# A two-block network on one core: the end of the first feed-forward, the place of memory's first key and value products, and the order inside three residual loops

## The chip, the core and the metric

One Trainium2 chip, one of its cores, one launch. The metric is the device time of the program in microseconds (us), lower is better. The core has five engines that each run their own instruction list and meet through semaphores: TensorE (PE) multiplies, VectorE (DVE), ScalarE (ACT) and GpSimd (POOL) do elementwise work, SyncE (SP) issues the weight loads.

## What is computed

Two blocks in a row on 256 tokens of width 1024, in float32. The first block ends with a feed-forward over a 3x3 convolution; the second has a mixer, an attention over 256 memory tokens, and a feed-forward. Cut to what matters here:

```python
# first block, its end
x = x + mx[:, :, 5] * conv_ffn(h2, ffn_up, ffn_conv_w, ffn_conv_b, ffn_down, rows, GRID_W)
x = rmsnorm(x, final_g)
# second block
h = rms_norm(x, norm_mix_w)
x = x + hybrid_mixer(h, w_in, pool_w, pool_scale, gk_w2, gk_b, gla_norm_w, w_out)
h = rms_norm(x, norm_xattn_w)
m = rms_norm(mem, norm_mem_w)
x = x + memory_cross_attention(h, m, wq, wkv, wo)     # keys m @ wk, values m @ wv
h = rms_norm(x, norm_ffn_w)
x = x + conv_ffn_2(h, w_up, conv_w, conv_b, w_down)
x = rms_norm(x, norm_final_w)
```

The keys and values of memory depend on `mem` alone, so their products can stand anywhere before the attention.

## The kernel before, in words

**Weights in two halves.** Every product is made of three TensorE passes, to keep float32's digits: high weights by high input, low weights by high input, high weights by low input. Weights come in chunks of 128x1024 (512 KB). `CHUNKS`, made by `chunk_list`, is their one order, and every engine follows it. SP loads chunk j into `raw`, ACT copies it, rounded, into `whi` (`splits`, line 1164), and DVE or POOL subtracts to get `wlo` (`low_half`, line 492; which of the two is `LOW_BY`). All three rings hold four chunks (`RAW`, `HL`): ACT may make the high half of chunk j only when TensorE has finished chunk j-4, and SP may load chunk j only when the low half of j-4 is made.

**One chunk on TensorE** is 24 matmuls: eight k tiles by three passes (`lin`, lines 625, 627, 629). `lins` takes three chunks side by side, one k tile after another. A feed-forward's down chunk (`slab`, lines 948 to 952) adds one k tile to all eight output columns, which lie in four banks; `slabs` does this for two chunks with the eight columns as the outer loop, so that the first columns are ready while the later ones are still being computed. `lin_tok` computes a chunk pair of the values with tokens as rows.

**Residual loops.** `residual(name)` runs over the eight columns j of a projection that is added to x. DVE adds the product to x (`xT`), ACT makes the high half of the next input (`h2h`, line 1388), DVE the low half (`h2l`, line 1572), ACT the squares (`sq`), DVE their sum (`ssum`). Between these stand the weights' halves of coming chunks. The names are `down` (end of the first feed-forward), `w_out2` (end of the mixer) and `wo` (end of the attention); the next products, `w_in2`, `wq` and `up2`, read `h2h` and `h2l` by k tile. The root mean square is not needed for these products: `means` sums the squares on TensorE, ACT takes the root, DVE inverts it, `spread` puts it on all partitions by a small matmul, and the products are scaled by it afterwards.

**Around the change.** TensorE ends the first feed-forward with down chunks 19 and 20 (counted from 0), memory's key columns 4 and 5 (`wk`), down chunk 21, and the pair of chunks of memory's values 0 (`wv`), then `w_in2`. Later, after the mixer's head products (lines 1058 and 1059), it takes the means of the heads (`g0`, `g1`), spreads the first block's root (`rs1`), computes key columns 6 and 7, spreads `mem`, and goes to `w_out2`. The last attention head is computed after the value chunks 6 and 7, and then `wo`.

## Time and profile before

| | |
|---|---|
| median of 3 runs | 893.72 us (891.81 to 894.41) |
| the profiled execution | 894.42 us |
| its span, first to last instruction | 892.6 us |
| PE, matmuls busy | 858.7 us (96%) |
| DVE busy | 583.2 us (65%) |
| ACT busy | 462.7 us (52%) |
| POOL busy | 441.5 us (49%) |
| mean granted TensorE clock | 0.985 |

The span is the part that the trace covers; 1.8 us of the profiled execution lie outside it. Matmul ends are modelled, so the spacing of their starts tells more than their busy time. A granted clock of 1.00 is TensorE's upper level (2.4 GHz), 0.50 the lower (1.2 GHz). A row's idle time, in square brackets, is what its engine waited before it, with the one that released it.

### The profile page before, as it was taken

How to read it: one execution, taken by the hardware profiler on the slowest of the kernel's cores; microseconds unless marked ns; L12 is line 12 of the kernel's file. 1: busy time of each engine (PE TensorE's matmuls, PEld its weight loads, DVE VectorE, ACT ScalarE, POOL GpSimd, SP SyncE). 2: the span in 40 equal slices, each digit the busy share in tenths (PEclk: the TensorE clock that was granted, in tenths of full speed). 3: DMA queues.
4: the chain of work that ended last, by engine and by line, in shares of the span. 5: the costliest groups of instructions: out<-in, count | busy, mean ns of one | idle time of the engine just before them, and what ended most of it. 6: DMA issues, size and time to landing. Idle time of an engine off the chain costs nothing.

```text
span 892.6 us, 16215 instructions
## 1 busy us (share of the span) xinstructions
PE 858.7 (96%) x6572; PEld 818.5 (92%) x6572; DVE 583.2 (65%) x1182; ACT 462.7 (52%) x753; POOL 441.5 (49%) x217
## 2 busy tenths in 40 slices
PE   6799999999999999999999899899999999999996
PEld 2388999998899999999999899899999999999996
DVE  6988987866767796776765769676458433433335
ACT  5332344542656665555554664455445555545555
POOL 0766412222652798888888100000003688787882
PEclk9899999999999999999999999899999999999998
DMA  9957574655375466565565446154535475655651
GB/s 344 350 210 247 181 236 163 225 166 185 134 239 187 145 191 192 182 189 184 176 187 182 134 127 204 53 167 133 174 98 163 123 211 181 187 177 186 189 166 48
DMA packets 45758, 160.95 MB, mean 180 GB/s; under 512 B 5218, under 2 KB 5490, under 8 KB 45556
## 3 DMA queue, kind: packets, MB, share of 16 engines
q1 hardware_dynamic: 45680, 159.91, 55.6%
q8 instruction: 52, 0.85, 0.4%
q14 instruction: 22, 0.18, 0.1%
q10 hardware_dynamic: 4, 0.01, 0.0%
HBM read 158.85 MB, written 1.05 MB: 179 GB/s over the span
## 4 chain that ended last, share of the span: by engine, by line
PE 78%; DVE 11%; ACT 4%; issue 3%; DMA 2%; POOL 1%; SPq 0%; DVEq 0%; ACTq 0%; POOLq 0%
PE bank L629 16%; PE bank L625 16%; PE bank L627 16%; PE bank L952 4%; PE bank L950 4%; PE bank L948 4%; DVE wlo L492 3%; ACT whi L1164 2%; PE bank L753 2%; PE bank L837 2%; DMA ada_kT<-in_adaT 1%; PE bank L705 1%; PE bank L694 1%; PE bank L690 1%; PE bank L692 1%
## 5 line engine op out<-in xcount | busy, mean ns | idle before, releaser
L492 POOL TENSOR_TENSOR wlo<-raw,whi 128x1024 fp32r<-128x1024 f32 (+1 forms) x177 | 411.9, 2348 | 392.2 <-ACT whi L1164 392.1
L1164 ACT ACTIVATE whi<-raw 128x1024 fp32r<-128x1024 f32 (+1 forms) x253 | 258.3, 1026 | 78.6 <-PE bank L629 41.7
L629 PE MATMUL bank<-h2l,whi 128*128 128x256 f32 x848 | 240.9, 284 | 2.4 <-DVE h2l L1572 2.4
L625 PE MATMUL bank<-h2h,whi 128*128 128x256 f32 x848 | 242.2, 286 | 0.5 <-ACT h2h L1388 0.5
L627 PE MATMUL bank<-h2h,wlo 128*128 128x256 f32 x848 | 240.4, 284 | 0.0
L1572 DVE SCALAR_TENSOR_TENSOR accs<-bank,vec,accs 128x189 f32<-128x189 f32 (+4 forms) x440 | 161.1, 432 | 72.3 <-ACT accs L1434 72.3
L629 PEld LDWEIGHTS bank<-h2l,whi 128*128 128x128 f32 x848 | 163.2, 192 | 3.5 <-DVE h2l L1572 3.5
L625 PEld LDWEIGHTS bank<-h2h,whi 128*128 128x128 f32 x848 | 163.3, 193 | 1.4 <-ACT h2h L1388 0.7
L627 PEld LDWEIGHTS bank<-h2h,wlo 128*128 128x128 f32 x848 | 163.3, 193 | 0.1
L492 DVE TENSOR_TENSOR wlo<-raw,whi 128x1024 fp32r<-128x1024 f32 x76 | 92.5, 1226 | 26.8 <-ACT whi L1164 26.3
L952 PE MATMUL bank<-gl,whi 128*128 128x256 f32 x336 | 95.2, 283 | 1.3 <-DVE gl L1569 1.3
L950 PE MATMUL bank<-gh,wlo 128*128 128x256 f32 x336 | 95.1, 283 | 0.0
L948 PE MATMUL bank<-gh,whi 128*128 128x256 f32 x336 | 95.1, 283 | 0.0
L1434 ACT ACTIVATE accs<-bank,vec 128x256 f32<-128x256 f32 x88 | 44.9, 561 | 86.7 <-DVE bank L1569 53.3
L1569 DVE TENSOR_TENSOR bank<-bank,rsd 128x256 f32<-128x256 f32 x44 | 16.8, 428 | 89.1 <-PE bank L629 89.1
L625 PE MATMUL bank<-hch,whi 128*128 128x256 f32 (+1 forms) x240 | 73.5, 306 | 0.0
L627 PE MATMUL bank<-hch,wlo 128*128 128x256 f32 (+1 forms) x240 | 73.0, 304 | 0.0
L629 PE MATMUL bank<-hcl,whi 128*128 128x256 f32 (+1 forms) x240 | 73.0, 304 | 0.0
L952 PEld LDWEIGHTS bank<-gl,whi 128*128 128x128 f32 x336 | 64.5, 192 | 1.5 <-DVE gl L1569 1.5
L948 PEld LDWEIGHTS bank<-gh,whi 128*128 128x128 f32 x336 | 64.5, 192 | 0.0
L950 PEld LDWEIGHTS bank<-gh,wlo 128*128 128x128 f32 x336 | 64.5, 192 | 0.0
L629 PEld LDWEIGHTS bank<-hcl,whi 128*128 128x128 f32 x240 | 45.8, 191 | 1.9
(328 smaller groups left out, 1689.0 us busy)
## 6 DMA issues: line engine op xcount, KB each, us to landing
raw<-in_up SPq DMA_DIRECT2D x88, 512.0 KB, 3.6
raw<-in_w_in SPq DMA_DIRECT2D x45, 512.0 KB, 3.7
raw<-in_down SPq DMA_DIRECT2D x44, 512.0 KB, 3.6
ada_kT<-in_adaT SPq DMA_DIRECT2D x22, 512.0 KB, 4.0
raw<-in_w_out SPq DMA_DIRECT2D x16, 512.0 KB, 4.3
raw<-in_w_in_t SPq DMA_DIRECT2D x12, 512.0 KB, 4.6
ada_vM<-in_adaT SPq DMA_DIRECT2D x10, 512.0 KB, 4.3
ada_buf<-in_adaT SPq DMA_DIRECT2D x8, 512.0 KB, 10.5
```

Source lines behind the costliest of these rows:

```text
L492: return e.tensor_tensor(wlo[:, j % HL, 0:k], raw[:, j % RAW, 0:k], whi[:, j % HL, 0:k].bitcast(F32), ALU.subtract)
L625: e.matmul(ps, wh[:, k, :], xh(k), start=k == 0, stop=False)
L627: e.matmul(ps, wl[:, k, :], xh(k), start=False, stop=False)
L629: t = e.matmul(ps, wh[:, k, :], xl(k), start=False, stop=k == KTILES[name] - 1)
L753: t = e.matmul(rows[h][0:2, :], M["cs"][:, k, :], M["ada_sc"][:, k, h * 512:h * 512 + 512], start=k == 0, stop=k == KT - 1)
L837: t = e.matmul(banks[4 + slot][:, h * 128:h * 128 + 128], M["near"][:, h, tile], by_blocks(Q2, h, tile, 1 << v), start=True, stop=True)
L948: e.matmul(ps, wh[:, j, :], gh, start=k == 0 and j % 2 == 0, stop=False, skip_group_check=True)
L950: e.matmul(ps, wl[:, j, :], gh, start=False, stop=False, skip_group_check=True)
L952: t = e.matmul(ps, wh[:, j, :], gl, start=False, stop=k == NFF - 1, skip_group_check=True)
L1164: e.activation(whi[:, j % HL, 0:(k1 - k0) * 128], raw[:, j % RAW, 0:(k1 - k0) * 128], ACT.Copy).then_inc(S.hi.up(j))
L1434: e.activation(acc_at(t), z_at(f, t), ACT.Identity, scale=conv_weight(f, n, centred(f)), bias=conv_bias(f, n)).then_inc(S.acc0.up((f, t)))
L1572: return e.scalar_tensor_tensor(out=out, in0=a, scalar=s, in1=b, op0=o1, op1=o2)
```

## The change

On TensorE, down chunks 20 and 21 are now computed together, by columns, with key column 4 ahead of them and key column 5 behind them; values 0 move from there to a place behind key column 7, before `w_out2`. The first `w_in2` chunks are computed one after another and not three side by side. The `rs1` spread and key column 6 go ahead of the heads' means, and DVE inverts their roots after it has scaled x. Part of the low halves changes engine: `w_in2` 16 goes from DVE to POOL, and `up2` 0, 22 and 1 from POOL to DVE. In the loops `w_out2` and `wo`, ACT makes the high half of chunk j+4 first, before it waits for the new x of column j, and DVE adds product j to x before the low half of chunk j+4, where that low half used to stand behind `h2l` of column j and ahead of the next addition. The last head's transposes (`turn(3)`) go between the two value chunks 6 and 7.

```diff
@@ chunk_list
-            elif i == NFF + DLAG - 1:
+            elif i == NFF + DLAG - 2:
                 for name, n in beside:
                     one(name, n)
...
-    ffn("up", "down", [("wk", 4), ("wk", 5)])
-    two("wv", 0)
+    ffn("up", "down", [("wk", 4)])
+    one("wk", 5)
...
     for j in (6, 7):
         one("wk", j)
+    two("wv", 0)
@@ low_by
-        if name in ("up", "down", "up2", "down2") or (name == "wk" and n in (4, 5)) or (name == "wv" and n < 2):
+        if name == "up2" and n in (0, 1, NFF):
+            out.append("dve")
+        elif name in ("up", "down", "up2", "down2") or (name == "wk" and n in (4, 5)) or (name == "wv" and n < 2):
+            out.append("pool")
+        elif (name, n) == ("w_in2", 16):
             out.append("pool")
@@ TensorE's list
-            for k in range(NFF - DLAG, NFF - 1):
-                slab(0, "down", k)
+            slab(0, "down", NFF - 3)
             mem_key(4)
+            slabs(0, "down", (NFF - 2, NFF - 1))
             mem_key(5)
-            slab(0, "down", NFF - 1)
-            mem_value(0)
...
-            for n in range(2):
-                means(f"g{n}", sq_at(("heads", 1, n)), 4, S.sqo, f"g{n}", (S.yb, (1, 2 * n + 1)), 1)
...
-            mem_key(6, lambda: [spread(f"g{n}", aux_bank(f"g{n}")) for n in range(2)])
-            mem_key(7)
+            mem_key(6)
+            for n in range(2):
+                means(f"g{n}", sq_at(("heads", 1, n)), 4, S.sqo, f"g{n}", (S.yb, (1, 2 * n + 1)), 1)
+            mem_key(7, lambda: [spread(f"g{n}", aux_bank(f"g{n}")) for n in range(2)])
+            mem_value(0)
...
-            mem_value(3)
-            turn(3)
+            mem_value(3, lambda: turn(3))
@@ ScalarE's residual
+                    if name in ("w_out2", "wo"):
+                        if j < 7:
+                            splits(ch(name, j) + HL + 1)
+                        else:
+                            sqrt_next()
                     if name in AHEAD:
...
-                        if j < 7:
-                            splits(ch(name, j + 1) + HL)
-                        if j == 7:
-                            sqrt_next()
                         squares(name, j, xT[:, j, :])
@@ VectorE's residual
-                        los(ch(name, j) + HL)
+                        if j == 0:
+                            los(ch(name, 0) + HL)
                         w.wait_ge(S.chunk, ch(name, j))
...
                         if name in AHEAD:
+                            if j < 7:
+                                los(ch(name, j) + HL + 1)
                             low(j)
```

**DVE in the residual loop `down`.** Rows of DVE's list, behind the last `gl` of the first feed-forward; `wlo` rows are weights' low halves. Before:

```order
L1572 SCALAR_TENSOR_TENSOR xT<-bank,mod,xT 128x256 [waits s_summed,s_ada]
L1572 SCALAR_TENSOR_TENSOR xT<-bank,mod,xT 128x256
L1572 SCALAR_TENSOR_TENSOR xT<-bank,mod,xT 128x256 [waits s_summed]
L1572 SCALAR_TENSOR_TENSOR h2l<-xT,fgm,h2h 128x256 [waits s_xh]
L1572 SCALAR_TENSOR_TENSOR xT<-bank,mod,xT 128x256
L1572 SCALAR_TENSOR_TENSOR h2l<-xT,fgm,h2h 128x256 [waits s_xh]
L1572 SCALAR_TENSOR_TENSOR xT<-bank,mod,xT 128x256 [waits s_summed]
L1572 SCALAR_TENSOR_TENSOR h2l<-xT,fgm,h2h 128x256 [waits s_xh]
L492 TENSOR_TENSOR wlo<-raw,whi 128x1024 [waits s_hi]
```

Now:

```order
L1579 SCALAR_TENSOR_TENSOR xT<-bank,mod,xT 128x256 [waits s_summed]
L1579 SCALAR_TENSOR_TENSOR xT<-bank,mod,xT 128x256
L1579 SCALAR_TENSOR_TENSOR h2l<-xT,fgm,h2h 128x256 [waits s_xh] x2
L1579 SCALAR_TENSOR_TENSOR xT<-bank,mod,xT 128x256 [waits s_chunk]
L1579 SCALAR_TENSOR_TENSOR xT<-bank,mod,xT 128x256
L1579 SCALAR_TENSOR_TENSOR h2l<-xT,fgm,h2h 128x256 [waits s_xh] x4
L497 TENSOR_TENSOR wlo<-raw,whi 128x1024 [waits s_hi]
L1576 TENSOR_TENSOR ssum<-ssum,sq 128x512 [waits s_sqr]
```

The additions now go in pairs with the low halves of the input in pairs behind them, and the weights' low half that stood among them (`w_in2` 16) is gone from DVE; the next one (`w_in2` 4) stands behind the last `h2l`.

**DVE from the memory keys into the loop `w_out2`.** Rows from the last products of the mixer's heads on. Before:

```order
L492 TENSOR_TENSOR wlo<-raw,whi 128x1024 [waits s_hi]
L1569 TENSOR_TENSOR ctl<-zb,cth 128x256 [waits s_cth] x2
L1569 TENSOR_TENSOR ctl<-az,cth 128x256 [waits s_cth] x2
L492 TENSOR_TENSOR wlo<-raw,whi 128x1024 [waits s_hi]
L1569 TENSOR_TENSOR kT<-kT,bank 128x2048 [waits s_spread,s_kT]
L492 TENSOR_TENSOR wlo<-raw,whi 128x1024 [waits s_hi,s_x2]
L1569 TENSOR_TENSOR xT<-bank,xT 128x256 [waits s_chunk]
L1572 SCALAR_TENSOR_TENSOR h2l<-xT,vec,h2h 128x256 [waits s_xh]
L492 TENSOR_TENSOR wlo<-raw,whi 128x1024 [waits s_hi]
```

Now:

```order
L1576 TENSOR_TENSOR ctl<-zb,cth 128x256 [waits s_cth] x2
L1576 TENSOR_TENSOR ctl<-az,cth 128x256 [waits s_cth] x2
L497 TENSOR_TENSOR wlo<-raw,whi 128x1024 [waits s_hi]
L1576 TENSOR_TENSOR kT<-kT,bank 128x2048 [waits s_spread,s_kT]
L497 TENSOR_TENSOR wlo<-raw,whi 128x1024 [waits s_hi,s_x2]
L497 TENSOR_TENSOR wlo<-raw,whi 128x1024 [waits s_hi] x2
L1576 TENSOR_TENSOR xT<-bank,xT 128x256 [waits s_chunk]
L497 TENSOR_TENSOR wlo<-raw,whi 128x1024 [waits s_hi]
L1579 SCALAR_TENSOR_TENSOR h2l<-xT,vec,h2h 128x256 [waits s_xh]
```

Three low halves (`w_out2` 1, 2 and 3) now stand behind the scaling of the keys (`kT`) and ahead of the first addition, where one stood; and in the loop the low half stands between the addition and `h2l`.

**TensorE from the heads' products to the memory keys.** Before, the heads' means (`ones,sq`) and the `rs1` spread stand ahead of key column 6:

```order
L1059 MATMUL bank<-A_149,V_147 128x256
L705 MATMUL bank<-ones,sq 128x1 [waits s_sqo]
L705 MATMUL bank<-ones,sq 128x1 x3
L713 MATMUL bank<-ident,rc 128x128 [waits s_inv,s_on]
L713 MATMUL bank<-ident,rc 128x128
L625 MATMUL bank<-mnh,whi 128x256 [waits s_hi,s_pooled]
```

Now:

```order
L1061 MATMUL bank<-A_149,V_147 128x256
L721 MATMUL bank<-ident,rc 128x128 [waits s_inv]
L721 MATMUL bank<-ident,rc 128x128
L630 MATMUL bank<-mnh,whi 128x256 [waits s_hi,s_pooled]
...
L634 MATMUL bank<-mnl,whi 128x256
L713 MATMUL bank<-ones,sq 128x1 [waits s_sqo]
```

The 24 matmuls of key column 6 now stand between the heads' products and the means that wait for ACT's squares.

## Rows read from the trace of the kernel before

**Rows 1.** The page: busy time, share of the span, instructions.

```profile
PE 858.7 (96%) x6572; PEld 818.5 (92%) x6572; DVE 583.2 (65%) x1182; ACT 462.7 (52%) x753; POOL 441.5 (49%) x217
```

**Rows 2.** Waits of TensorE: us in total, times, longest us.

```profile
PE bank L645 <- ACT whi L1164: 3.5, 1, 3.5
PE bank L705 <- ACT sq L1324: 2.5, 1, 2.5
PE bank L629 <- DVE h2l L1572: 2.4, 3, 1.7
...
PE bank L952 <- DVE gl L1569: 1.3, 1, 1.3
```

**Rows 3.** Windows: busy us (matmuls) of PE, PEld, DVE, ACT, POOL; clock; DMA.

```profile
498.90:507.10 8.20, 4.43 (x23) 4.06 (x22) 6.50 (x10) 8.13 (x19) 2.47 (x4) 0.79 0.56 167
...
566.10:575.40 9.30, 6.84 (x32) 6.48 (x31) 4.09 (x12) 4.34 (x8) 0.00 (x0) 0.63 0.17 56
...
582.40:605.20 22.80, 22.80 (x192) 22.80 (x192) 17.69 (x26) 11.90 (x20) 0.00 (x0) 1.00 0.50 162
...
690.80:698.30 7.50, 5.75 (x34) 5.38 (x33) 2.52 (x4) 3.94 (x7) 6.04 (x3) 0.77 0.45 134
```

**Rows 4.** Timeline of DVE, end of the first feed-forward.

```profile
491.36 1.27 DVE L1572 SCALAR_TENSOR_TENSOR xT<-bank,mod,xT 128x256 f32<-128x256 f32 x3 [8.11 <-PE bank L952]
...
498.76 1.27 DVE L1572 SCALAR_TENSOR_TENSOR h2l<-xT,fgm,h2h 128x256 fp32r<-128x256 f32 x3
```

**Rows 5.** Timeline of ACT, the same place.

```profile
500.00 0.40 ACT L1187 ACTIVATE sq<-xT 128x256 f32<-128x256 f32 x1
500.30 0.49 ACT L1189 ACTIVATE sq<-xT,vec 128x256 f32<-128x256 f32 x1
...
506.26 1.28 ACT L1178 ACT_TABLE_LOAD   x1
```

**Rows 6.** Timeline of TensorE: the means and spread of `down`.

```profile
516.25 0.95 PE L705 MATMUL bank<-ones,ssum 128*128 128x1 f32 x8
...
518.22 0.67 PE L713 MATMUL bank<-ident,rc 128*128 128x128 f32 x4
```

**Rows 7.** Timeline of DVE there, and ahead of the heads' means.

```profile
517.24 0.16 DVE L1968 COPY rc<-bank 128x2 f32<-128x2 f32 x1 [0.39 <-PE bank L705]
...
564.86 1.23 DVE L492 TENSOR_TENSOR wlo<-raw,whi 128x1024 fp32r<-128x1024 f32 x1 [0.52 <-ACT whi L1164]
```

**Rows 8.** Timeline of ACT ahead of the heads' means.

```profile
566.89 1.28 ACT L1178 ACT_TABLE_LOAD   x1
...
568.29 1.07 ACT L1324 ACTIVATE sq<-bank 128x512 f32<-128x512 f32 x2
```

**Rows 9.** Timeline of DVE: key scaling and one column of the loop `w_out2`.

```profile
582.50 2.29 DVE L1569 TENSOR_TENSOR kT<-kT,bank 128x2048 f32<-128x2048 f32 x1 [0.67 <-PE bank L713]
...
585.84 0.42 DVE L1569 TENSOR_TENSOR xT<-bank,xT 128x256 f32<-128x256 f32 x1
...
587.78 1.23 DVE L492 TENSOR_TENSOR wlo<-raw,whi 128x1024 fp32r<-128x1024 f32 x1 [0.46 <-ACT whi L1164]
588.92 0.42 DVE L1569 TENSOR_TENSOR xT<-bank,xT 128x256 f32<-128x256 f32 x1
```

**Rows 10.** Timeline of ACT, the same column.

```profile
586.71 1.04 ACT L1164 ACTIVATE whi<-raw 128x1024 fp32r<-128x1024 f32 x1
```

**Rows 11.** Timeline of POOL: low halves at either feed-forward.

```profile
479.71 4.72 POOL L492 TENSOR_TENSOR wlo<-raw,whi 128x1024 fp32r<-128x1024 f32 x2 [0.36 <-ACT whi L1164]
...
682.62 4.96 POOL L492 TENSOR_TENSOR wlo<-raw,whi 128x1024 fp32r<-128x1024 f32 x2 [180.59 <-ACT whi L1164]
```

**Rows 12.** Timeline of DVE at the end of the loop `wo`.

```profile
682.68 0.42 DVE L1569 TENSOR_TENSOR xT<-bank,xT 128x256 f32<-128x256 f32 x1 [0.57 <-PE bank L629]
683.02 2.29 DVE L1569 TENSOR_TENSOR ssum<-ssum,sq 128x256 f32<-128x256 f32 x1
685.24 2.62 DVE L1572 SCALAR_TENSOR_TENSOR h2l<-xT,vec,h2h 128x256 fp32r<-128x256 f32 x1
```

More of the change, by code:

```diff
@@ L696, in lin_tok @@
                     t.then_inc(S.chunk.up(c))
+                    if between and half == 0:
+                        between()
             def means(key, src, n, signal, event, until, by=0):
@@ L1441, in ffn @@
                         cut(f, i - 1)
-                for k in range(NFF - DLAG, NFF - 1):
-                    splits(ch(down, k) + HL)
+                splits(ch(down, NFF - 3) + HL)
                 silu(f, NFF - 1)
@@ L1939, in residual @@
                     if name == "down":
-                        if j > 1:
+                        if j > 1 and j % 2:
+                            low(j - 3)
                             low(j - 2)
-                        if j == 4:
-                            los(ch("w_in2", 16) + 1)
-                        if j == 6:
-                            los(ch("w_in2", 4) + 1)
                     else:
```

44 lines of the change are left out of this document (23 added, 21 removed).

## The prediction, made before the changed kernel had run

> **What bounds the kernel now.** I read the page first, then TensorE's waits, then windows around each long wait, then the timelines of the engines that feed it. The page shows TensorE busy for 96% of the span, the others for 49 to 65% [rows 1]. So only what TensorE loses can be won: waits, and time at the lower clock. The waits that the edits touch are four [rows 2]: 3.5 us before `w_in2` behind the high half of a weight; 2.5 us before the heads' means behind ACT's squares; 2.4 us in three pieces behind `h2l`, the longest 1.7 us; 1.3 us in down chunk 20 behind `gl`. The other large ones lie at the start of the program, where nothing changes. The windows show that waits cost twice [rows 3]: behind three of these four the granted clock falls. In a full stretch 192 matmuls take 22.8 us, 0.12 us each. From 498.9 to 507.1 us the mean clock is 0.79, which is (1 - 0.79) x 8.2 = 1.7 us lost to the lower level beside the idle time; from 566.1 to 575.4 it is 0.63, so 3.4 us; from 690.8 to 698.3 it is 0.77, so 1.7 us. The 1.3 us wait at 481 us is followed by no fall.
>
> **The change part by part.** I name four places.
>
> *A, end of the first feed-forward.* Lost now: the `gl` wait, 1.3 us and some 0.1 around it, and the stretch 498.9 to 507.1, in which about 21 of the 23 matmuls listed start: 8.2 - 21 x 0.12 = 5.7 us. Together 7.1 us. Key column 4 (24 x 0.12 = 2.9 us) now stands in front of down chunk 20 and covers the `gl` wait. With down 20 and 21 by columns (5.8 us), the first two output columns are final 1.4 us into the pair, and DVE can begin its additions about 4.4 us ahead of the pair's end. What is between the pair's end and the end of the old place's idle time: key column 5, 2.9 us, then `w_in2` 16, whose last `h2l` is needed 2.8 us further on. I follow the engines on the old clock. The pair runs from 483.0 to 488.8, key column 5 to 491.7. DVE adds at 0.40 us apiece, and an `h2l` takes 0.40 us too [rows 4]. Sixteen of them take 6.4 us from 484.7 on, were nothing in the way.
>
> Something is. POOL makes the low halves of `wk` 5 and `w_in2` 16 at 2.4 us each [rows 11], from about 483.8 to 488.6. At the loop `wo` the trace shows what such an overlap does: while POOL makes two low halves, the addition that reads PSUM takes 0.42 us, but `ssum`, usually 0.4 us, takes 2.29 and an `h2l` 2.62 us [rows 12], each ending with POOL's instruction [rows 11]. All three operands of those lie in SBUF. The first `h2l` in the loop `down` will meet the same: it is due at 487.0 and ends at 488.9. By these rows the last `h2l` comes at about 493.3; without an overlap it would be 491.8. The Trainium skill, page "SBUF — State Buffer", section "SBUF: two separate sides", says that a DVE instruction with two SBUF inputs and a GpSimd instruction that reads SBUF hold one pair of ports in turn, the second blocked until the first is done. By that rule the trace agrees (2.29 and 2.62 us against 0.4).
>
> TensorE still does not wait for `h2l`, since `w_in2` 16 asks for the last at 494.4. But ACT is pushed back by 1.5 us too, and it has these in front of the root mean square: three high halves of 1.04 us [rows 10], seven pairs of squares at 0.7 us and the table load of 1.28 us [rows 5]. I get the last square at 502.8 and its sum at 503.5, where TensorE, through with `w_in2` 6, comes to the means at 503.2. Then the low halves of `w_in2` 7 and 0 stand in front of DVE's copy of the sum. It copies at 505.8; TensorE could spread 0.98 us later as before [rows 6, 7], at 506.7, and would be there at 505.1. The waits: 0.4 + 0.2 + 1.1 = **1.7 us new**. Key column, values, products and DVE's work behind the spread move with it. The bounds are 0.2 us (no overlap, all slack kept) and 3.2 us (one more overlap of 2.4 us on the chain, of which 0.9 us of slack is eaten). A is worth -7.1 + 1.7 = -5.4 us.
>
> *B, heads.* Lost now: 2.5 us of wait and 3.4 us of low clock, 5.9 us [rows 2, 3]. The chain is the low half of `w_out2` 0 on DVE (1.23 us), the product `rg` behind it [rows 7], a table load of 1.28 us and the squares [rows 8]. In the new chunk order values 0 stand at this point, on POOL, so DVE's low half is gone from the chain: the squares come 1.6 us earlier. And TensorE has the `rs1` spread (0.5 us) and key column 6 (2.9 us) to do, 3.4 us against a wait that would be 0.9. Then the means come, DVE scales eight columns of x (0.4 us each) before it inverts, and the spread inside key column 7 may come 0.2 us late. B: -5.9 + 0.2 = **-5.7 us**. Values 0 cost 5.8 us here and are saved in A. Their low halves on POOL (two of 2.4 us) meet DVE instructions that read PSUM.
>
> *C, the loop `w_out2`.* DVE now has three low halves behind the scaling of the keys (2.29 us), which itself waits for the `mem` spread just ahead of `w_out2` [rows 9]. That of `w_out2` 1 is ready 3.6 us after the spread, TensorE wants it 2.9 us after: **0.7 us new**. The first addition comes 2.4 us later than before. In exchange the cycle is shorter. Now it is 3.08 us from addition to addition [rows 9], against TensorE's 2.88: addition, `h2h`, high half, low half, next addition hang in one chain. Afterwards the high half hangs on TensorE's chunk alone, and DVE needs 0.4 + 0.4 + 1.2 + 0.4 = 2.4 us a column, so it catches up within four or five columns. The waits at the end of this loop (the rest of the three `h2l` pieces and 0.5 us for `h2h`, under 1 us) go. C: 0.0 us, between -0.8 and +1.5.
>
> *D, `turn(3)`.* The values' last chunk ends 0.5 us later for the transposes in its middle, and the mixing waits for the copy of just those values. It moves the wait and saves nothing: 0.0 us.
>
> *E, the loop `wo`.* Lost now: 1.7 us of wait behind `h2l`, about 0.2 around it, 1.7 us of low clock, 3.6 us [rows 2, 3]. Its cause is again POOL: two `ssum` and one `h2l` take 2.3 to 2.6 us each while POOL makes `up2` 0, 22 and 1 [rows 11, 12]. These low halves are DVE's now, 1.2 us each, and fit in the 2.88 us column. POOL starts again with `up2` 23, behind the last `h2l`. The table load for the root now stands ahead of the last `h2h`, where ACT idles. E: -3.6 + 0.1 = **-3.5 us**.
>
> **Sum.** -5.4 - 5.7 + 0.0 + 0.0 - 3.5 = -14.6 us. One thing more: the waits of 1.7 us in A lie within 3.6 us of each other, with the means' eight small matmuls between them [rows 6]. Of the waits now, 1.7 us was followed by the lower clock and 1.3 us was not [rows 2, 3], so I take it that one stretch of low clock returns, at the price that either short one has now, 1.7 us. That makes **-12.9 us** on the profiled execution of 894.4: 881.5. The median lies 0.7 us under the profiled execution: **880.8 us**.
>
> **The rivals.** *All clear:* A's new waits stay too short for the lower clock, or do not come. For it: no wait up to 1.3 us cost clock. Against it: POOL's overlap is seen three times in three at `wo`. -14.6 gives 879.1, without A's waits -16.3 gives 877.4. Chance 0.30.
>
> *The gain is partly given back at B or E:* B's sixteen means and sixteen spread matmuls keep the clock low although nobody waits (+3.4, 884.2), or E's wait stays (+3.5, 884.3), because the last `h2h` waits behind a table load of 1.28 us. For it: B has much small work in little time. Against it: the means and spread from 516 to 519 us had no fall behind them [rows 6]. Chance 0.23.
>
> *Slower:* the new order on DVE makes the loops slower than before. The place is the low half that stands between the addition and `h2l`; if ACT makes the high half only after the previous column's `h2h` and squares, DVE sits in front of it with x unsplit. Each column above 2.88 us costs TensorE its excess; 16 columns eat 13 us when the column takes 2.88 + 0.81 = 3.7 us. From there on the kernel is slower. At 4.0 us it would be 18 us more, 898.7. Against it: DVE's four instructions of a column add to 2.4 us and ACT's three to 1.9. Chance 0.02. The change also does nothing if the waits only move to the next stage; but DVE's own chain starts behind the same spread and moves with it. Chance 0.03 of within 0.3%, which is about what a measurement of this kernel can tell from no change.
>
> *The forecast*, about 881, has the rest, 0.42.
>
> **How the numbers follow.** Low end: the all-clear case with C at its best, 877.4 - 0.8, about 876.5. High end: forecast with A at its upper bound (+1.5) and C at its upper bound (+1.5) is 883.8, the given-back case 884.3; with both a little more, 886. Faster by over 0.3% (under 891.0): 0.95; same 0.03; slower 0.02.
>
> **What would show it.** Right: no wait over 0.2 us between 478 and 503 us; the first `h2l` of `down` at over 1.5 us; key column 6 directly behind the heads' products with no wait before the means; a wait of 0.6 to 0.8 us behind `wlo` in `w_out2` 1; additions 2.9 us apart at the loops' ends; `ssum` and `h2l` in `wo` at 0.4 and 0.5 us; one stretch of low clock near 505 us and none at 570 or 695. Wrong: a wait for a weight's low or high half in `w_in2` 4 to 6, where my slack is 0.2 to 0.5 us; a fall of the clock near 560; additions over 2.9 us apart.

## The result and the profile after

The changed kernel takes 880.28 us (median of 4 runs, 879.90 to 880.94), the kernel before beside it 892.76 us (890.38 to 894.41): ratio 0.9855, 95% interval 0.9834 to 0.9875. The profiled execution took 880.59 us, its span 878.8. Forecast were 880.8 us and a range of 876.5 to 886.0.

The page's busy line, which answers to [rows 1]:

```profile
PE 852.7 (97%) x6572; PEld 813.2 (93%) x6572; DVE 579.3 (66%) x1184; ACT 461.7 (53%) x753; POOL 436.9 (50%) x215
```

TensorE's waits between 290 and 862 us (us in total, times, longest; waits from 0.15 us on are listed, and the smallest, 0.2, is left out here), which answer to [rows 2]:

```profile
PE bank L1107 <- ACT vM L1222: 1.0, 1, 1.0
PE bank L634 <- DVE h2l L1579: 0.7, 2, 0.4
PE bank L721 <- DVE rc L1594: 0.7, 1, 0.7
PE bank L632 <- DVE wlo L497: 0.6, 1, 0.6
PE bank L696 <- issue: 0.6, 1, 0.6
PE bank L713 <- DVE ssum L1576: 0.4, 1, 0.4
```

The waits of 3.5, 2.5, 1.7 and 1.3 us are gone. New are 0.4 us before the means of `down` (`ssum`), 0.7 before their spread (`rc`) and 0.6 behind `wlo` in `w_out2` 1. The 1.0 us behind `vM` is the last attention head's; before, a wait of the same size stood there behind `PT`. The two pieces behind `h2l` stand at 297 us, in front of the first feed-forward, which no edit touches: of the "three pieces" in [rows 2] only the longest was the loop `wo`'s.

Windows around the places whose clock had fallen in [rows 3] (the first, second and last line), and over the loop `w_out2` (the third) (PE, PEld, DVE, ACT, POOL busy us; clock; DMA):

```profile
503.80:509.80 6.00, 4.88 (x39) 4.50 (x38) 4.53 (x11) 3.64 (x7) 0.00 (x0) 1.00 0.51 167
555.40:564.80 9.40, 9.40 (x81) 9.35 (x81) 6.61 (x19) 4.16 (x11) 3.49 (x2) 1.00 0.20 56
571.60:594.40 22.80, 22.20 (x185) 22.00 (x184) 20.13 (x29) 13.79 (x24) 0.00 (x0) 1.00 0.59 193
679.80:687.30 7.50, 7.46 (x63) 7.25 (x62) 2.28 (x7) 3.89 (x7) 4.68 (x3) 1.00 0.47 140
```

The clock is 1.00 in all of them, also in the first, where the prediction had one stretch of the lower level return.

DVE's timeline at the end of the first feed-forward, answering to [rows 4, 7], then POOL's, answering to [rows 11]:

```profile
487.70 2.37 DVE L1579 SCALAR_TENSOR_TENSOR h2l<-xT,fgm,h2h 128x256 fp32r<-128x256 f32 x2
...
492.36 1.66 DVE L1579 SCALAR_TENSOR_TENSOR h2l<-xT,fgm,h2h 128x256 fp32r<-128x256 f32 x4
...
505.47 1.22 DVE L497 TENSOR_TENSOR wlo<-raw,whi 128x1024 fp32r<-128x1024 f32 x1
506.60 0.15 DVE L1976 COPY rc<-bank 128x2 f32<-128x2 f32 x1
```

```profile
484.62 4.77 POOL L497 TENSOR_TENSOR wlo<-raw,whi 128x1024 fp32r<-128x1024 f32 x2 [1.71 <-ACT whi L1166]
```

The first two `h2l` take 2.37 us together, the last four 1.66. The first one takes 1.97 us of it and ends at 489.7, 0.3 us behind POOL's second low half (489.4). And DVE's copy of the sum, for which TensorE's spread waits, stands behind the low half of `w_in2` 0.

DVE in the loop `w_out2` (as [rows 9]) and at the end of `wo` (as [rows 12]), in one view:

```profile
571.88 2.29 DVE L1576 TENSOR_TENSOR kT<-kT,bank 128x2048 f32<-128x2048 f32 x1 [4.31 <-PE bank L721]
574.08 3.49 DVE L497 TENSOR_TENSOR wlo<-raw,whi 128x1024 fp32r<-128x1024 f32 x3
577.49 0.42 DVE L1576 TENSOR_TENSOR xT<-bank,xT 128x256 f32<-128x256 f32 x1
...
674.21 0.42 DVE L1576 TENSOR_TENSOR xT<-bank,xT 128x256 f32<-128x256 f32 x1
674.55 0.42 DVE L1576 TENSOR_TENSOR ssum<-ssum,sq 128x256 f32<-128x256 f32 x1
...
677.09 0.42 DVE L1576 TENSOR_TENSOR xT<-bank,xT 128x256 f32<-128x256 f32 x1
...
678.09 0.48 DVE L1579 SCALAR_TENSOR_TENSOR h2l<-xT,vec,h2h 128x256 fp32r<-128x256 f32 x1 [0.24 <-ACT h2h L1395]
```

At the end of `wo` additions are 2.88 us apart (674.21, 677.09), `ssum` and `h2l` take 0.4 and 0.5 us.

**Where the time went, by stage.** A program's first microseconds vary, so I compare distances between TensorE's starts inside one trace: from the first `up` matmul of the first feed-forward (294.29 us before, 295.10 after) to the first matmul of `w_in2_t`, of `w_out2`, of `wq`, of `wo`, of `up2`, and to the last means. The distances of all kernels, in us:

| kernel | to `w_in2_t` | to `w_out2` | to `wq` | to `wo` | to `up2` | to the end | sum |
|---|---|---|---|---|---|---|---|
| before | 239.72 | 48.14 | 23.11 | 59.76 | 23.22 | 195.86 | 589.81 |
| after | 228.26 | 48.17 | 23.96 | 58.18 | 23.22 | 192.36 | 574.15 |
| loops_only | 240.23 | 48.34 | 23.11 | 58.19 | 23.22 | 192.36 | 585.45 |
| up2_dve | 239.69 | 48.16 | 23.11 | 59.75 | 23.22 | 195.96 | 589.89 |
| up2_pool | 228.26 | 48.14 | 23.97 | 58.19 | 23.22 | 192.90 | 574.68 |
| loops_old | 228.25 | 48.16 | 23.97 | 64.00 | 23.22 | 196.01 | 583.61 |
| table_first | 228.25 | 48.17 | 23.97 | 62.47 | 23.22 | 193.05 | 579.13 |
| means_first | 228.97 | 50.41 | 23.97 | 58.19 | 23.21 | 192.36 | 577.11 |
| values_early | 235.89 | 43.87 | 23.12 | 58.18 | 23.21 | 192.36 | 576.63 |
| wait_1 | 230.20 | 47.95 | 23.97 | 58.18 | 23.21 | 192.36 | 575.87 |
| wait_2 | 232.17 | 47.68 | 23.97 | 58.17 | 23.22 | 192.35 | 577.56 |
| in16_dve | 227.73 | 48.17 | 23.96 | 58.18 | 23.22 | 192.35 | 573.61 |
| improved | 228.41 | 48.16 | 23.12 | 55.38 | 24.76 | 192.36 | 572.19 |
| best | 226.73 | 48.17 | 23.11 | 55.40 | 24.76 | 192.36 | 570.53 |

Each row is one execution. Stages that no edit touches mostly repeat within 0.03 us, far finer than the medians; where they do not, the lower clock fell otherwise in them or ahead of them (the first two columns of loops_only, means_first, wait_1 and wait_2). The values' two chunks (48 matmuls at 0.12, 5.76 us) stand in the first column before and in the second after. So A is -11.46 + 5.76 = -5.70, B +0.03 - 5.76 = -5.73, C and D (+0.85 - 1.58) -0.73, E -3.50: together -15.66 us. The spans differ by 13.8 only: the first `up` matmul came 0.81 us later, and 9.56 us lie behind the last means against 8.53. In all 14 traces those two ends lie between 294.0 and 297.5 and between 8.0 and 9.6 us, in no order that follows an edit.

### The profile page after: what moved, and what is told of

Same layout as the page of the kernel before. It is cut to its first block, busy times and chain, and to the rows that moved or that the text cites. A ratio compares the mean times of both kernels' runs of the same rounds, so it can differ in the third digit from the quotient of the medians.

```text
span 878.8 us, 16212 instructions
## 1 busy us (share of the span) xinstructions
PE 852.7 (97%) x6572; PEld 813.2 (93%) x6572; DVE 579.3 (66%) x1184; ACT 461.7 (53%) x753; POOL 436.9 (50%) x215
## 3 DMA queue, kind: packets, MB, share of 16 engines
HBM read 158.85 MB, written 1.05 MB: 182 GB/s over the span
## 4 chain that ended last, share of the span: by engine, by line
PE 90%; DVE 3%; ACT 2%; DMA 2%; POOL 1%; issue 1%; SPq 0%; DVEq 0%; POOLq 0%; ACTq 0%
PE bank L630 19%; PE bank L634 19%; PE bank L632 19%; PE bank L958 4%; PE bank L956 4%; PE bank L960 4%; PE bank L696 3%; PE bank L700 3%; PE bank L698 3%; PE bank L761 2%; PE bank L845 2%; POOL wlo L497 1%; PE bank L721 1%; DMA ctxT<-in_ctxT 1%; PE bank L1086 1%
## 5 line engine op out<-in xcount | busy, mean ns | idle before, releaser
L497 POOL TENSOR_TENSOR wlo<-raw,whi 128x1024 fp32r<-128x1024 f32 (+1 forms) x175 | 406.9, 2344 | 385.5 <-ACT whi L1166 385.4
L630 PE MATMUL bank<-h2h,whi 128*128 128x256 f32 x872 | 248.3, 285 | 0.0
L634 PE MATMUL bank<-h2l,whi 128*128 128x256 f32 x872 | 247.0, 283 | 0.7 <-DVE h2l L1579 0.7
L632 PE MATMUL bank<-h2h,wlo 128*128 128x256 f32 x872 | 246.8, 283 | 0.0
L634 PEld LDWEIGHTS bank<-h2l,whi 128*128 128x128 f32 x872 | 167.3, 192 | 1.3 <-DVE h2l L1579 1.3
L630 PEld LDWEIGHTS bank<-h2h,whi 128*128 128x128 f32 x872 | 167.3, 192 | 0.7 <-issue 0.3
L956 PE MATMUL bank<-gh,whi 128*128 128x256 f32 x320 | 90.6, 283 | 0.0
L958 PE MATMUL bank<-gh,wlo 128*128 128x256 f32 x320 | 90.6, 283 | 0.0
L960 PE MATMUL bank<-gl,whi 128*128 128x256 f32 x320 | 90.6, 283 | 0.0
L632 PEld LDWEIGHTS bank<-hch,wlo 128*128 128x128 f32 x240 | 45.8, 191 | 1.9
```

Of the source, the lines that this page charges most:

```text
L497: return e.tensor_tensor(wlo[:, j % HL, 0:k], raw[:, j % RAW, 0:k], whi[:, j % HL, 0:k].bitcast(F32), ALU.subtract)
L630: e.matmul(ps, wh[:, k, :], xh(k), start=k == 0, stop=False)
L632: e.matmul(ps, wl[:, k, :], xh(k), start=False, stop=False)
L634: t = e.matmul(ps, wh[:, k, :], xl(k), start=False, stop=k == KTILES[name] - 1)
L956: e.matmul(ps, wh[:, j, :], gh, start=k == 0 and j % 2 == 0, stop=False, skip_group_check=True)
L958: e.matmul(ps, wl[:, j, :], gh, start=False, stop=False, skip_group_check=True)
```

## The experiments

Medians are given with their ratio to runs of the kernel before that were made beside them, with its 95% interval; against the changed kernel I read the table. The text ahead of each result is what was expected before the run.

**The loops alone.** The kernel before, with ScalarE's and VectorE's new order in `w_out2` and `wo` and with `up2` 0, 22 and 1 on DVE.

```diff
@@ ScalarE's residual, in the kernel before
+                    if name in ("w_out2", "wo"):
+                        if j < 7:
+                            splits(ch(name, j) + HL + 1)
+                        else:
+                            sqrt_next()
...
-                        if j < 7:
-                            splits(ch(name, j + 1) + HL)
-                        if j == 7:
-                            sqrt_next()
@@ VectorE's residual
-                        los(ch(name, j) + HL)
+                        if j == 0:
+                            los(ch(name, 0) + HL)
...
+                            if j < 7:
+                                los(ch(name, j) + HL + 1)
                             low(j)
@@ low_by
+        if name == "up2" and n in (0, 1, NFF):
+            out.append("dve")
```

> The kernel before, with only the loops w_out2 and wo in their new order and the low halves of up2 0, 22 and 1 on DVE. My sum: E is worth -3.5 us, and C's gain (-0.8) comes without its new wait, since no values stand ahead of w_out2 here; together -4.3 us against the kernel before. Additions 2.9 us apart, no h2l wait at the end of wo, no low clock behind it. Rival, that the low clock after wo does not hang on the 1.7 us wait: only the wait goes, -2 to -2.7 us. Rival, that the loops' gain needs the earlier stages changed too: within 1 us of before.

889.07 us (10 runs), 0.9959 (0.9941 to 0.9976). By the table -4.36 us: -1.57 between `wq` and `wo`, -3.50 behind `up2`, and +0.71 ahead of `w_out2`, where nothing is edited. That +0.71 is the clock's: behind the wait of 3.5 us this trace has clock 0.50 from 501.7 to 508.6 us, the kernel before only from 503.7 to 507.1, and at the heads the level fell 0.3 us behind the end of the wait, where before it fell 0.4 us ahead of it and so was in part idle time. So C's gain is 1.6 and not 0.8 us, and -4.3 as a whole fits only by that +0.7. `turn(3)` is in its old place here, and the stage that holds it takes 58.19 against the changed kernel's 58.18: D is 0.0.

**Only the engine of three low halves.**

```diff
@@ low_by, in the kernel before
+        if name == "up2" and n in (0, 1, NFF):
+            out.append("dve")
```

> The kernel before with one edit: the low halves of up2 0, 22 and 1 on DVE and not on POOL; the loops keep their old order. The prediction's cause for E (POOL holds DVE's ssum and h2l, and that makes the wait) gives -3.5 us against the kernel before. The cause that the earlier runs point to (the order in the loop: additions 3.08 us apart, the table load ahead of the last squares) gives 0.0 us, between -0.5 and +0.5: the wait of 1.7 us behind h2l becomes one of about 1.5 us before the means behind ssum, and the low clock stays.

895.63 us (12 runs), 1.0011 (0.9996 to 1.0025); by the table +0.08 us. Nothing is won. TensorE's waits from 650 to 700 us and DVE's timeline at the end of `wo`:

```profile
PE bank L707 <- DVE ssum L1571: 1.5, 1, 1.5
```

```profile
692.89 0.42 DVE L1571 TENSOR_TENSOR xT<-bank,xT 128x256 f32<-128x256 f32 x1
693.22 0.41 DVE L1571 TENSOR_TENSOR ssum<-ssum,sq 128x256 f32<-128x256 f32 x1
693.88 0.48 DVE L1574 SCALAR_TENSOR_TENSOR h2l<-xT,vec,h2h 128x256 fp32r<-128x256 f32 x1 [0.25 <-ACT h2h L1390]
695.70 0.43 DVE L1571 TENSOR_TENSOR ssum<-ssum,sq 128x256 f32<-128x256 f32 x1 [1.33 <-ACT sq L1189]
```

The collisions of [rows 12] are gone (`ssum` 0.41, `h2l` 0.48), and so is the wait of 1.7 us behind `h2l`; in its place TensorE waits 1.5 us before the means, for a sum whose squares ACT makes behind its table load. The lower clock stays too (0.78 from 694.4 to 702.0 us). The prediction named POOL as the cause of E; taking POOL away does not move the time.

**The reverse.** `up2` 0, 22 and 1 back on POOL in the changed kernel.

```diff
@@ low_by
-        if name == "up2" and n in (0, 1, NFF):
-            out.append("dve")
```

> The changed kernel with the low halves of up2 0, 22 and 1 back on POOL. Theory of the prediction, that POOL alone makes E's wait: the wait behind h2l returns, with the low clock +3.5 us against the changed kernel. Rival, from following the engines in the changed kernel's rows: with the high half ahead of h2h, POOL's three low halves each hold one h2l or ssum for about 2 us, every addition from column 5 on is some 0.8 us late, yet the last h2l comes near 679.3 us where TensorE wants it at 679.7; then 0 to +0.5 us, with the collisions to be seen and no wait.

879.27 us (5 runs), 0.9844 (0.9817 to 0.9870); by the table +0.53 us against the changed kernel. DVE in `wo`, then POOL beside it:

```profile
668.90 2.33 DVE L1577 SCALAR_TENSOR_TENSOR h2l<-xT,vec,h2h 128x256 fp32r<-128x256 f32 x1 [0.79 <-ACT h2h L1393]
...
671.49 2.62 DVE L1574 TENSOR_TENSOR ssum<-ssum,sq 128x256 f32<-128x256 f32 x1
674.03 0.47 DVE L1577 SCALAR_TENSOR_TENSOR h2l<-xT,vec,h2h 128x256 fp32r<-128x256 f32 x1
```

```profile
668.55 2.40 POOL L495 TENSOR_TENSOR wlo<-raw,whi 128x1024 fp32r<-128x1024 f32 x1 [105.14 <-ACT whi L1164]
671.43 2.40 POOL L495 TENSOR_TENSOR wlo<-raw,whi 128x1024 fp32r<-128x1024 f32 x1 [0.48 <-ACT whi L1164]
```

The collisions are back, one a column, and the clock stays up. No wait of 0.15 us or more follows, but the 0.53 us is lost at the loop's end all the same: matched matmul by matmul with the changed kernel, TensorE is on time up to the last k tile of `up2` 0, and its next few starts slip by 0.1 to 0.3 us each. With the high half ahead of `h2h` the loop has slack for all but this.

**The old order.** ACT's and DVE's loops as in the kernel before, all else as changed.

```diff
@@ ScalarE's residual
-                    if name in ("w_out2", "wo"):
-                        if j < 7:
-                            splits(ch(name, j) + HL + 1)
-                        else:
-                            sqrt_next()
...
+                        if j < 7:
+                            splits(ch(name, j + 1) + HL)
+                        if j == 7:
+                            sqrt_next()
@@ VectorE's residual
-                        if j == 0:
-                            los(ch(name, 0) + HL)
+                        los(ch(name, j) + HL)
...
-                            if j < 7:
-                                los(ch(name, j) + HL + 1)
```

> The changed kernel with ACT's and DVE's old order in the loops w_out2 and wo, and up2 0, 22, 1 left on DVE. Theory that the order carries it: additions 3.08 us apart; in w_out2 the first addition is 2.4 us late and the loop never catches up, so its end waits 3.3 us, with low clock 5.0; wo ends with a wait of some 0.4 us: +3.7 to +5.5 us against the changed kernel. Rival, that only the engine of the three up2 low halves matters: 0 to +1 us.

889.26 us (10 runs), 0.9946 (0.9929 to 0.9963); by the table +9.46 us against the changed kernel, 5.82 of it ahead of `wo` and 3.65 behind. Waits from 560 to 700 us, and windows over the two clock falls:

```profile
PE bank L630 <- ACT h2h L1390: 1.9, 1, 1.9
PE bank L713 <- DVE ssum L1575: 1.5, 1, 1.5
```

```profile
599.60:608.80 9.20, 9.14 (x47) 8.76 (x48) 4.05 (x7) 4.13 (x7) 0.00 (x0) 0.63 0.51 147
685.30:693.00 7.70, 6.21 (x36) 5.86 (x36) 0.60 (x3) 3.73 (x7) 4.70 (x2) 0.78 0.42 128
```

(1 - 0.63) x 9.2 = 3.4 us and (1 - 0.78) x 7.7 = 1.7 us of lower level stand behind these waits. In `w_out2`, where the loop starts late behind the scaling of the keys, the old order would have lost 5.8 us, where it lost 1.6 in the kernel before. In `wo` it brings back all of E, with the three low halves on DVE. The expected +3.7 to +5.5 was far too little: at `wo` a wait of 0.4 us without a fall of the clock was expected, and there came 1.5 us with one.

**The old order with the table load first.** As loops_old, with

```diff
@@ ScalarE's residual
+                    if name in ("w_out2", "wo") and j == 7:
+                        sqrt_next()
```

> As loops_old (the changed kernel with the old order in the loops w_out2 and wo), but with ACT's table load ahead of the last h2h, as in the changed kernel. Theory: the old cycle of 3.08 us makes the loop wo end late, and the table load behind the last h2h turns that into the wait of 1.5 us before the means and the low clock; with the load first the stage wo is 0.3 us over the changed kernel's 26.5 us and no low clock follows it. The loss in w_out2 (5.8 us in loops_old) stays: +6 us against the changed kernel, -3.4 against loops_old. Rival, that the cycle alone makes the wait: same as loops_old.

885.94 us (6 runs), 0.9919 (0.9894 to 0.9944); by the table -4.48 us against loops_old. Its windows at the same two places:

```profile
600.90:608.00 7.10, 7.04 (x42) 6.67 (x43) 4.00 (x7) 4.03 (x6) 0.00 (x0) 0.76 0.53 150
685.30:693.00 7.70, 7.66 (x62) 7.44 (x63) 2.41 (x8) 4.32 (x8) 5.05 (x3) 1.00 0.50 156
```

In `wo` no listed wait and no low clock are left: of the 3.65 us the place of the table load alone is worth 2.96, the rest of the order 0.69 (both with the low halves of `up2` 0, 22 and 1 on DVE; with them on POOL it was not run). In `w_out2` the wait of 1.9 us behind `h2h` stays, and half of the low clock goes, -1.53 us, which was not expected. No run shows whether that hangs on the table load's place or is the clock's chance.

**Means first.** TensorE takes the heads' means ahead of the `rs1` spread and key column 6, DVE inverts each ahead of scaling x, as before.

```diff
@@ TensorE's list
+            for n in range(2):
+                means(f"g{n}", sq_at(("heads", 1, n)), 4, S.sqo, f"g{n}", (S.yb, (1, 2 * n + 1)), 1)
...
             spread("rs1", banks[4 + slot])
-            mem_key(6)
-            for n in range(2):
-                means(f"g{n}", sq_at(("heads", 1, n)), 4, S.sqo, f"g{n}", (S.yb, (1, 2 * n + 1)), 1)
-            mem_key(7, lambda: [spread(f"g{n}", aux_bank(f"g{n}")) for n in range(2)])
+            mem_key(6, lambda: [spread(f"g{n}", aux_bank(f"g{n}")) for n in range(2)])
+            mem_key(7)
@@ VectorE's list
+                if h % 2:
+                    inverse(f"g{h // 2}")
             second_x()
-            for n in range(2):
-                inverse(f"g{n}")
```

> The changed kernel with the heads' means (and their inversion on DVE) ahead of key column 6, as before, the rs1 spread behind them. A wait of 0.9 to 1.0 us before the means. If waits of this size leave the clock alone, as the changed kernel's 1.1 us at the means of down did: +1.0 us and clock 1.00. Rival, that the small matmuls of the heads, the wait and the means together lower the clock: +2.7 us with one short stretch of it, +4.3 with one as long as before.

881.35 us (6 runs), 0.9858 (0.9832 to 0.9884); by the table +2.96 us in the profiled execution, 0.71 at A and 2.24 at B. Waits from 480 to 600 us, and two windows, at A and at B:

```profile
PE bank L721 <- DVE rc L1594: 0.7, 1, 0.7
PE bank L713 <- ACT sq L1326: 0.6, 1, 0.6
...
PE bank L713 <- DVE ssum L1576: 0.4, 1, 0.4
```

```profile
503.10:509.10 6.00, 4.89 (x31) 4.51 (x30) 4.04 (x9) 3.28 (x6) 0.00 (x0) 0.79 0.52 157
555.20:564.50 9.30, 8.67 (x60) 8.30 (x59) 7.04 (x20) 4.31 (x11) 3.45 (x2) 0.82 0.33 95
```

At B a wait of 0.6 us was followed by the lower level, for (1 - 0.82) x 9.3 = 1.7 us, so key column 6 in front of the means is worth its place. The rival named this case, and a wait of 0.9 to 1.0 where 0.6 came. And at A, where this kernel does the same as the changed one and waits the same 0.4 and 0.7 us, the clock fell too (0.79). It is not settled by the waits alone: of the five traces with these waits at A (after, up2_pool, loops_old, table_first, means_first) it fell in one. The six executions of this kernel had mean clocks from 0.989 (the profiled one) to 0.993, so its median holds less of it than the trace.

**Values early.** Values 0 back in front of `w_in2`, behind key column 5, ScalarE's and VectorE's lists shifted with them.

```diff
@@ chunk_list
     one("wk", 5)
+    two("wv", 0)
...
-    two("wv", 0)
@@ TensorE's list
             mem_key(5)
+            mem_value(0)
...
-            mem_value(0)
@@ ScalarE's residual, down
                         if j == 5:
-                            splits(ch("w_in2", 4) + 1)
+                            splits(ch("wv", 1) + 1)
                         if j == 7:
-                            splits(ch("w_in2", 5) + 1)
+                            splits(ch("w_in2", 16) + 1)
...
-                        if j in (2, 5):
-                            splits(ch("w_in2", 6 + j // 5) + 1)
+                        if j == 2:
+                            splits(ch("w_in2", 4) + 1)
+                        if j == 5:
+                            mem_value(0)
+                            splits(ch("w_in2", 5) + 1)
@@ VectorE's residual, down
-                        if j in (1, 4):
-                            los(ch("w_in2", 5 + j // 4) + 1)
+                        if j == 5:
+                            los(ch("w_in2", 5) + 1)
```

> The changed kernel with values 0 back in front of w_in2, behind key column 5 (the pair of down chunks by columns and all else stay). If the move of the values was no part of the gain: A's waits before the means and the spread (1.1 us) go, as 5.8 us more stand in front of them, and C's wait of 0.6 us goes, as fewer low halves stand behind the scaling of the keys: -1.7 us against the changed kernel. Rival, that the values are needed as cover at B: the ctl of the last heads comes 1 to 2 us late in w_out2 0, +1 to +3 us with the clock.

885.49 us (5 runs), 0.9897 (0.9877 to 0.9918); by the table +2.48 us: A +1.87, B +1.46, C -0.84. Waits from 480 to 600 us, and DVE ahead of the heads' squares:

```profile
PE bank L632 <- POOL wlo L497: 1.7, 1, 1.7
PE bank L721 <- DVE rc L1596: 1.2, 1, 1.2
```

```profile
564.12 1.23 DVE L497 TENSOR_TENSOR wlo<-raw,whi 128x1024 fp32r<-128x1024 f32 x1 [0.52 <-ACT whi L1166]
565.26 0.42 DVE L1578 TENSOR_TENSOR rg<-bank,rsd 128x256 f32<-128x256 f32 x1
568.27 0.87 DVE L1581 SCALAR_TENSOR_TENSOR zb<-bank,vec,rg 128x256 f32<-128x256 f32 x2 [2.60 <-ACT sq L1326]
```

Both expected gains came (no wait before the means or the spread of `down`, none behind `wlo` in `w_out2`), and more was lost. At A the low half of `w_in2` 16 stands fourth in POOL's list and comes 1.7 us late. At B the low half of `w_out2` 0 stands on DVE ahead of `rg` again, and TensorE waits 1.2 us for the heads' spread. The rival was right on B, with another wait than it named.

**Longer waits at A.** DVE makes the low half of `w_in2` 0 once (wait_1) or twice (wait_2) more than needed.

```diff
@@ VectorE's list, ahead of the copy of the sum
+            los(ch("w_in2", 7) + 1)
+            w.wait_ge(S.hi, ch("w_in2", 0))
+            for _ in range(1):                      # wait_2: range(2)
+                low_half(e, ch("w_in2", 0)).then_inc(own())
+                w.wait_ge(own_dve, own_dve.n)
```

> The changed kernel; DVE makes the low half of w_in2 0 twice ahead of its copy of the sum, the first one of no use. The wait before the spread goes from 0.71 to about 1.95 us, 0.4 us before the means as before. Without a fall of the clock +1.25 us; with one at the price of a short stretch (the prediction's term, 1.7) +2.95; the changed kernel itself showed none at waits of 0.4 and 0.7 us.

> As wait_1, with two useless low halves: the wait before the spread about 3.2 us. Without a fall of the clock +2.5 us; with a short stretch +4.2, with a long one (3.4, as behind the 2.5 us wait of the kernel before) +5.9. Theory: falls, since every wait of 1.7 us and more in the kernel before was followed by one.

882.14 us (6 runs), 0.9870 (0.9844 to 0.9896), and 883.34 us (6 runs), 0.9883 (0.9858 to 0.9907); by the table +1.72 and +3.41 us. The waits before the spread were 1.97 and 3.23 us. Windows from the means on, of wait_1 and then of wait_2:

```profile
504.10:512.30 8.20, 5.83 (x35) 5.46 (x34) 6.20 (x12) 4.20 (x7) 0.00 (x0) 0.79 0.44 136
```

```profile
503.30:514.50 11.20, 7.57 (x41) 6.92 (x40) 9.17 (x15) 4.79 (x7) 0.00 (x0) 0.70 0.31 98
```

The clock fell in both. By the windows that is (1 - 0.79) x 8.2 = 1.7 and (1 - 0.70) x 11.2 = 3.4 us. Yet beside the added waits (1.26 and 2.52 us) only 0.46 and 0.89 us are left by the table. Matched matmul by matmul with the changed kernel, wait_1 is 2.7 us late right behind the stretch, 1.9 at the first `w_in2_t` matmul and 1.7 at `w_out2`; wait_2 4.6, 3.9 and 3.4. So three things make the difference.

- The window sums count the lower level also where TensorE stands idle, and there it costs nothing. In wait_2 it began at 507.5 us, 2.0 us before the wait ended. What TensorE lost by it was 2.7 - 1.26 = 1.4 us in wait_1 and 4.6 - 2.52 = 2.1 us in wait_2.
- At the first `w_in2_t` matmul 0.7 us come back in both, and in means_first too. The changed kernel waits 0.6 us there, and these three do not.
- The last 0.2 and 0.5 us come back at the mixer's scores, behind it.

The wait at `w_in2_t` is named "issue" in the list, for a release that the profile does not show. The rows and the program say what it is. TensorE's row first, then DVE's:

```profile
523.36 0.36 PE L696 MATMUL bank<-whi,h2h 128*128 128x256 f32 x1 [0.58 <-issue]
```

```profile
522.04 1.22 DVE L497 TENSOR_TENSOR wlo<-raw,whi 128x1024 fp32r<-128x1024 f32 x1
```

This is the low half of `w_in2_t` 0, for which the matmul waits in the program. It ends at 523.26, and the matmul starts 0.10 us later. The same 0.10 us stands between the two in all eleven traces that have this wait; in wait_1, wait_2 and means_first the low half ended 0.3 to 0.9 us before the matmul's turn. In the changed kernel DVE is the later one here, so TensorE can lose 0.7 us ahead of this place at no cost, as long as DVE is not made late by it.

**`w_in2` 16 on DVE.**

```diff
@@ low_by
-        elif (name, n) == ("w_in2", 16):
-            out.append("pool")
@@ VectorE's residual, down
                             low(j - 2)
+                            if j == 5:
+                                los(ch("w_in2", 16) + 1)
```

> The changed kernel with the low half of w_in2 16 on DVE (1.2 us, behind the low halves of the input columns 2 and 3) and not on POOL. The first h2l of down takes 0.5 and not 2.0 us. What DVE wins there (1.5 us) it pays back with 1.2 of its own: 0.0 us, between -0.4 and +0.4. If the prediction was right that POOL's overlap costs the waits before the means and the spread (1.1 us), they shrink by 0.3 us at most; rival, that they hang on ACT's chain and do not move.

878.78 us (4 runs), 0.9839 (0.9816 to 0.9862); by the table -0.54 us. DVE in `down`:

```profile
486.69 0.87 DVE L1577 SCALAR_TENSOR_TENSOR h2l<-xT,fgm,h2h 128x256 fp32r<-128x256 f32 x2
```

The gain is a little above what was expected (-0.4 at most). The first two `h2l` take 0.87 us where they took 2.37, the wait of 0.4 before the means is gone, and the one of 0.71 before the spread stays to the hundredth: that one does not hang on the collision, but on the low half in front of the copy.

**Three repairs.** The changed kernel, with

```diff
@@ VectorE's list
-            los(ch("w_in2", 5) + HL)
+            los(ch("w_in2", 7) + 1)
             w.wait_ge(S.total, "down")
...
-            los(ch("wk", 7) + HL)
+            los(ch("wk", 7) + HL + 1)
@@ TensorE's list: k 0 to 5 of wo's columns 0 and 1, mix(3) between them, then k 6 and 7 of both
-            mix(3)
-            residual("wo", of("oh", "ol", ...))
+            residual("wo", of("oh", "ol", ...), 2, 6, lambda: mix(3))
```

> The changed kernel with three repairs. DVE copies the sum of down ahead of the low half of w_in2 0: the wait of 0.71 us before the spread goes. DVE makes the low half of w_out2 1 ahead of the scaling of the keys: the 0.60 us wait in w_out2 goes. TensorE does k 0 to 5 of wo's first two columns around the last head's mixing: the 1.02 us wait for ACT's copy of the values goes. Together -2.3 us against the changed kernel's rows; about 878. Rival, that the first additions of wo come 2 us later for it and the loop ends late: the third repair is worth 0 or less, -1.3 in all.

877.62 us (4 runs), 0.9828 (0.9805 to 0.9852); by the table -1.96 us: `w_out2` -0.84, the last head -1.26 (-2.80 + 1.54, as some of `wo` now stands ahead of its mixing), and A +0.15, where -0.7 was expected. At A the 0.71 us wait went, but a wait of 0.36 us for the low half of `w_in2` 3 came, and the one at `w_in2_t` grew from 0.58 to 1.09: -0.71 + 0.36 + 0.51 = +0.16. DVE there:

```profile
507.21 0.35 DVE L1595 RECIPROCAL rc<-rc 128x2 f32<-128x2 f32 x2 [0.36 <-ACT rc L1173]
508.61 0.41 DVE L1577 TENSOR_TENSOR glow<-bank,rsd 16x256 f32<-16x256 f32 x1 [1.05 <-ACT rsd L1177]
...
509.29 1.20 DVE L497 TENSOR_TENSOR wlo<-raw,whi 128x1024 fp32r<-128x1024 f32 x1
```

The low half went from in front of the copy to behind the first scalings, past a gap of 1.05 us that it could have filled. From there on DVE is late, and TensorE's two new waits are waits for DVE's low halves. The last run fills the gap:

```diff
@@ improved and in16_dve together, and in VectorE's list
             inverse("rs1")
+            los(ch("w_in2", 5) + HL)
             w.wait_ge(S.by_row, "rsd")
```

> The three repairs of improved, with the low half of w_in2 16 on DVE as in in16_dve, and DVE's low half of w_in2 0 put between its inversion of the root and the copy of the spread, where it was idle for 1.05 us. In improved that low half came after the first scalings, which made DVE late for w_in2 3 (0.36 us) and gave back part of the 0.71. Theory: from down chunk 17 to the end improved is 2.0 us shorter than the changed kernel; in16_dve adds 0.5 (the wait before the means goes), the better place 0.4 to 0.8: -2.9 to -3.3 us, about 877. Rival, that DVE's low half delays the copy of the spread or that the issue wait of TensorE before the next chunks grows by what is won (1.09 us in improved, 0.58 in the changed kernel): -2.0 to -2.5.

876.01 us (5 runs), 0.9800 (0.9785 to 0.9815), the fastest here; by the table -3.62 us against the changed kernel, A -1.53. That is 0.3 us more than the most that was expected, and this rest is not explained. TensorE's listed waits between 290 and 862 us:

```profile
PE bank L632 <- DVE h2l L1578: 0.7, 2, 0.4
PE bank L696 <- issue: 0.6, 1, 0.6
PE bank L1086 <- DVE qT L1575: 0.2, 1, 0.2
```

## Why the prediction was right, and where it was not

**The number.** 880.8 against 880.28. The sum -14.6 was the step that was nearly right (-15.66 by the table). The step behind it failed: "I take it that one stretch of low clock returns", +1.7 us. The changed kernel's trace has no such stretch; its case was the rival *all clear*. That the end result still fits is chance: in the profiled execution the first feed-forward began 0.81 us later and the part behind the last means took 1.03 us longer than in the one before, 1.8 us which no term foresaw and which stand where the 1.7 us were put.

**The clock.** The reason given for that term (a wait of 1.7 was followed by the lower level, one of 1.3 was not) is too simple. The same two waits of 0.4 and 0.7 us left it up in four traces and not in a fifth, a wait of 0.6 at the heads let it fall, one of 1.97 and one of 3.23 did. The price at A was mis-sized too: TensorE loses 1.4 us in the stretch, of which 0.7 come back where it would have waited for DVE at `w_in2_t`, so 0.7 us are left there (means_first) and 0.5 by `w_out2` (wait_1), not 1.7. At `wo` it is nearly full: loops_old loses 3.65 us there, with a wait of 1.5 and 1.7 us of low clock in its windows.

**A**, -5.4 forecast, -5.70 measured. The chain went as written: the first `h2l` held up to 0.3 us behind the end of POOL's low half, the last one at 494.0, no wait in `w_in2` 16 to 6. The new waits were 0.4, 0 and 0.7, for 0.4, 0.2 and 1.1. in16_dve splits them: 0.4 is the collision's, 0.7 the copy's place on DVE. They are 0.6 us shorter in sum than forecast and the stage only 0.3 us better, so 0.3 of the 7.1 us that the old place was said to lose did not come back. values_early shows that the values had to go: left in front of `w_in2`, the three low halves ahead of `w_in2` 16 on POOL cost 1.7 us.

**B**, -5.7 and -5.73. Both parts that it named were needed: means_first shows the one (key column 6 in front of the means), values_early the other (values and not `w_out2` 0 where DVE makes `rg`).

**C**, 0.0 forecast, -0.73 measured. The new wait came (0.60 for 0.7) at its place, with 0.85 us lost in the stage. The gain was mis-sized: 1.6 and not 0.8 us (loops_only). I had counted two `h2l` pieces that stand elsewhere, and left out what a wait for `h2h` costs around itself. What the forecast missed altogether is what the new order protects: with the late start of the loop the old order loses 5.8 us here. The parts of the change are therefore not additive: the loops alone are worth 4.4 us, all else alone 589.81 - 583.61 = 6.2, and both 15.7 (the three low halves of `up2` are on DVE in either part). Of the 5.1 us between, 5.8 - 1.6 = 4.2 are this loop's and 0.7 the clock's chance in loops_only.

**D**, 0.0 and 0.0, as written: the wait moved from `PT` to `vM` and kept its 1.0 us.

**E**, -3.5 and -3.50, for a wrong reason. "Its cause is again POOL" fails twice, by up2_dve (the collisions gone, nothing won, +0.08 us) and up2_pool (the collisions back, 0.53 of the 3.50 us lost). In the old order two chains end at the same place: `h2l` 7 behind the collisions, and the last squares behind the table load. Take away the first, and TensorE waits 1.5 us for the second. The prediction gave the table load half a sentence; its place alone is worth 2.96 us (table_first against loops_old). What was wrong was the path and not the price: either chain costs about the same (a wait of 1.7 or 1.5 us and the same stretch of clock), and the change happened to shorten both, so the number came out right by luck.

**The rivals.** Nothing was given back at B or E. *Slower* had its mechanism at a column of 3.7 us; in `wo` the columns are at TensorE's 2.88.

## What to carry to other kernels

A wait has a last releaser, but often a second one close behind it: before a collision or a late buffer is called the cause, take it away in the old kernel and see whether the time moves or only the releaser's name. Follow the chain to the next consumer too (here the means behind the product), with table loads counted as instructions of the chain. And where a loop starts late, its slack for each column decides what that costs, so edits that shift work in front of a loop and edits that shorten its cycle have to be costed together.
